# Feed-forward stages of a two-block transformer kernel: gate and up products with the weights stationary

## The reference, cut to what matters

```python
h = rms_norm(x, norm2_g[l])                      # x * rsqrt(mean(x^2) + eps) * g
x = x + (jax.nn.silu(h @ w_gate[l]) * (h @ w_up[l])) @ w_down[l]     # D_FF = 2816
```

## Time and profile before

| | us |
|---|---|
| three runs | 1618.80, 1624.56, 1621.87 |
| median | 1621.87 |
| the profiled execution, its own time | 1621.89 |
| its span, first to last instruction | 1620.1 |
| mean granted TensorE clock | 0.994 of full |

### The profile page before, as it was taken

One profiled execution on the slowest core, in us unless ns is written; L12 is line 12 of the kernel. 1 busy time (PEld: TensorE's weight loads), 2 busy tenths in 40 slices (PEclk: granted clock), 3 DMA queues, 4 the chain that ended last, 5 costly groups with the idle time before them and its releaser, 6 DMA issues.

```text
span 1620.1 us, 18657 instructions
## 1 busy us (share of the span) xinstructions
PE 1581.8 (98%) x7684; PEld 1312.0 (81%) x7684; DVE 1059.0 (65%) x1321; ACT 773.4 (48%) x887; POOL 29.1 (2%) x24
## 2 busy tenths in 40 slices
PE   8999999999999999899998999999999998999997
PEld 6888888888888888788886888888888886788886
DVE  5778565666875657955556876567955556875655
ACT  5645444456554445654344354445554444354443
POOL 0100000001000000000100000000000010000000
PEclk9999999999999999999999999999999999999999
DMA  8535555454355554444633454554543633365551
GB/s 306 180 107 198 189 197 186 156 192 146 132 206 184 195 189 161 180 156 133 167 130 113 168 188 182 185 195 166 204 150 134 149 130 130 132 219 182 184 195 63
DMA packets 54243, 273.78 MB, mean 169 GB/s; under 512 B 18704, under 2 KB 19344, under 8 KB 22160
## 3 DMA queue, kind: packets, MB, share of 16 engines
q1 hardware_dynamic: 40496, 268.05, 46.3%
q10 hardware_dynamic: 13664, 4.55, 2.0%
HBM read 271.53 MB, written 1.05 MB: 168 GB/s over the span
## 4 chain that ended last, share of the span: by engine, by line
PE 81%; DVE 11%; ACT 5%; issue 2%; DMA 0%; ACTq 0%; DVEq 0%; PEldq 0%
PE psum L391 24%; PE psum L393 24%; PE psum L392 24%; DVE wl L1211 5%; PE psum L431 3%; ACT wh L863 3%; PE psum L764 1%; PE psum L485 1%; DVE arena L1335 1%; PE psum L738 1%; ACT arena L1112 1%; PE psum L770 1%; DVE work L1300 1%; DVE arena L1293 1%; DVE work L1671 1%
## 5 line engine op out<-in xcount | busy, mean ns | idle before, releaser
L1211 DVE TENSOR_TENSOR wl<-raw,wh 128x2048 fp32r<-128x2048 f32 x250 | 573.6, 2298 | 424.8 <-ACT wh L863 421.6
L391 PE MATMUL psum<-wh,xh 128*128 128x512 f32 (+1 forms) x1632 | 648.4, 397 | 4.9 <-DVE work L1671 1.8
L393 PE MATMUL psum<-wh,xl 128*128 128x512 f32 (+1 forms) x1632 | 634.3, 389 | 0.0
L392 PE MATMUL psum<-wl,xh 128*128 128x512 f32 (+1 forms) x1632 | 633.3, 388 | 0.0
L863 ACT ACTIVATE wh<-raw 128x2048 fp32r<-128x2048 f32 x250 | 476.1, 1910 | 321.7 <-PE psum L393 315.2
L391 PEld LDWEIGHTS psum<-wh,xh 128*128 128x128 f32 x1632 | 308.0, 189 | 77.2 <-issue 19.3
L393 PEld LDWEIGHTS psum<-wh,xl 128*128 128x128 f32 x1632 | 307.6, 189 | 63.4
L392 PEld LDWEIGHTS psum<-wl,xh 128*128 128x128 f32 x1632 | 308.2, 189 | 58.0
L391 PE MATMUL psum<-wh,ah 128*128 128x512 f32 (+1 forms) x360 | 141.7, 394 | 6.4 <-DVE work L1671 6.4
L393 PE MATMUL psum<-wh,al 128*128 128x512 f32 (+1 forms) x360 | 140.9, 391 | 0.0
L392 PE MATMUL psum<-wl,ah 128*128 128x512 f32 (+1 forms) x360 | 140.8, 391 | 0.0
(11 more groups left out here) (156 smaller groups left out, 1075.2 us busy)
## 6 DMA issues: line engine op xcount, KB each, us to landing
raw<-in_weights SPq DMA_DIRECT2D x250, 1024.0 KB, 4.8
arena<-in_rpb ACTq DMA_DIRECT2D x32, 96.0 KB, 6.6
raw<-in_weights SPq DMA_DIRECT2D x8, 256.0 KB, 7.5
out<-arena SPq DMA_DIRECT2D x3, 256.0 KB, 3.0
x<-in_x SPq DMA_DIRECT2D x2, 256.0 KB, 3.5
x<-in_x ACTq DMA_DIRECT2D x2, 256.0 KB, 7.0
arena<-in_table_decay SPq DMA_DIRECT2D x1, 512.0 KB, 5.1
work<-in_masks SPq DMA_DIRECT2D x1, 512.0 KB, 5.2
```

The source lines that it names most:

```text
L391: nc.tensor.matmul(dst, lh, right(wh, slot), start=start, stop=False)
L392: nc.tensor.matmul(dst, lh, right(wl, slot), start=False, stop=False)
L393: return nc.tensor.matmul(dst, ll, right(wh, slot), start=False, stop=stop)
L1211: nc.vector.tensor_tensor(wl[:, slot, :], raw[:, slot, :], wh[:, slot, :].bitcast(F32), ALU.subtract).then_inc(split_ready.sem, 1)
```

## The change

- Gate and up are transposed. A 128 x 128 block of the weights is stationary and the tokens stream past: `wh` against `xh` and `xl` side by side (512 columns, two strips of 256 from the joint tile `xhl`, into the left and the right half of a bank), then `wl` against `xh` (256 columns, into the left half). The result is left plus right half, with hidden features on the partitions, in four chunks c: gate in the two PROJ banks, up in the two TR banks (for slice 0 in ACC+2 and ACC+3). The transposes and their bank are gone.
- The activation changes with it. ScalarE copies the gate's right halves, VectorE adds the left halves (which frees PROJ), multiplies by the norm's factor, ScalarE takes tanh, VectorE makes `(tanh + 1) * gate`; ScalarE copies the up halves, VectorE adds and multiplies. `ah` and `al` are made from the result in SBUF.
- The factor now varies along a row. VectorE builds diagonals from it, TensorE multiplies a matrix of ones by them (`rms_rows`, one f32 matmul of 256 columns inside `gate_up` of slice 0), and VectorE copies the row tile `rms_row`. The factor of the up product, with the 0.5, is applied after down, in `add_to_x` (`scaled=True`).
- Orders: VectorE does `split_low(F+3)` before `activate(0)`, ScalarE loads the tanh table with a one-element activation and does `split_high(F+3)` before the slice's copies; in each turn `act_high` and `act_low` come before the split of piece q+3.

The signal counts, the memset of `ones` and the changed calls are left out of this diff:

```diff
-xh = sb("xh", [P, KT, SEQ], F32R)
-xl = sb("xl", [P, KT, SEQ], F32R)
+xhl = sb("xhl", [P, 2, KT, SEQ], F32R)
+xh, xl = xhl[:, 0, :, :], xhl[:, 1, :, :]
...
-mlp_gate = part(work, 0, NT, 256)
-mlp_tanh = part(work, 1024, NT, 256)
-mlp_act = part(work, 1536, NT, 256)
+mlp_gate = part(work, 0, 2, SEQ)
+rms_row, rms_diag = part(work, 512, SEQ), part(work, 768, SEQ)
+mlp_tanh = part(work, 1024, 2, SEQ)
+mlp_act = part(work, 1536, 2, SEQ)
+mlp_up = part(work, 4096, 2, SEQ)
...
+def up_banks(i):
+    return TR if i else ACC + 2
+def halves(first):
+    return psum[:, first:first + 2, 0:SEQ], psum[:, first:first + 2, SEQ:2 * SEQ]
...
     def ffn(L, F, U, xl_groups, norm_n, after):
-        def gate_up(i, q, slot, groups=(None, None), between=None):
-            project(L, q, U + i, 0, last=False, slot=slot, left_ready=groups[0], between=between)
-            yield
-            project(L, q + 1, U + i, 4, first=False, slot=(slot + 1) % RING,
-                    left_ready=groups[1])
-        def act_t(i):
-            pe.wait_ge(*a_ready.by(L, i + 1))
-            for kk in range(2):
-                for t in range(NT):
-                    mm = nc.tensor.transpose(bank(TR)[:, kk * SEQ + t * P:kk * SEQ + (t + 1) * P],
-                                             mlp_act[:, t, kk * P:(kk + 1) * P], ident[:, :])
-            mm.then_inc(at_full.sem, 1)
+        def gate_up_half(i, q, k0, slot, groups=None, between=None):
+            pe.wait_ge(*split_ready.by(L, q + 1))
+            for c in range(4):
+                if k0 == 0 and c % 2 == 0:
+                    pe.wait_ge(*proj_free[c // 2].by(L, U + i))
+                if (i, k0, c) == (1, 0, 2):
+                    pe.wait_ge(*tr_free.by(L, norm_n + 4))
+                dst = bank((up_banks(i) if c >= 2 else PROJ) + c % 2)
+                for kk in range(4):
+                    if groups is not None and c == 0 and kk % 2 == 0:
+                        pe.wait_ge(*xl_ready.by(L, groups + kk // 2 + 1))
+                    cols = slice(kk * 512 + c * P, kk * 512 + (c + 1) * P)
+                    nc.tensor.matmul(dst, wh[:, slot, cols], xhl[:, :, k0 + kk, :],
+                                     start=(k0, kk) == (0, 0), stop=False, skip_group_check=True)
+                    mm = nc.tensor.matmul(dst[:, 0:SEQ], wl[:, slot, cols], xh[:, k0 + kk, :],
+                                          start=False, stop=(k0, kk) == (4, 3), skip_group_check=True)
+                if c == 1:
+                    if k0 == 4:
+                        mm.then_inc(proj_full[0].sem, 1)
+                    if between:
+                        between()
+            mm.then_inc(piece_used.sem, 1)
+        def gate_up(i, q, slot):
+            gate_up_half(i, q, 0, slot)
+            gate_up_half(i, q + 1, 4, (slot + 1) % RING)
+        def rms_rows():
+            pe.wait_ge(*diag_ready.by(L, 1))
+            nc.tensor.matmul(bank(ACC)[:, 0:SEQ], ones[:, :], rms_diag, start=True, stop=True)\
+                .then_inc(row_full.sem, 1)
...
-            act_t(i)
...
+                pe.wait_ge(*proj_free[1].by(L, U + FFI))
...
         def turn(i, q, start):
-            g = gate_up(i, q, (F + 2) % RING)
-            next(g)
-            act_t(i - 1)
-            for _ in g:
-                pass
+            gate_up(i, q, (F + 2) % RING)
             down(i - 1, q + 2, (F + 4) % RING, start)
-        for _ in gate_up(0, F, F % RING, (xl_groups - 4, xl_groups - 2),
-                         lambda: norm_operand(L, norm_n, 4, (2, 3))):
-            pass
+        gate_up_half(0, F, 0, F % RING, xl_groups - 4, lambda: norm_operand(L, norm_n, 4, (2, 3)))
+        gate_up_half(0, F + 1, 4, (F + 1) % RING, xl_groups - 2, rms_rows)
         turn(1, F + 2, True)
         for i in range(2, FFI - 1):
             turn(i, i * 3 + (F - 1), False)
         last = FFI - 1
-        g = gate_up(last, F + 29, (F + 29) % RING)
-        next(g)
-        act_t(last - 1)
-        for _ in g:
-            pass
+        gate_up(last, F + 29, (F + 29) % RING)
         last_downs(last, F + 31)
...
-    def ffn(L, F, U, rms_n, after):
-        def gate_tanh(i, full1):
-            for t in range(NT):
-                act.wait_ge(*(full1 if t else proj_full[0].by(L, U + i + 1)))
-                nc.scalar.activation(mlp_tanh[:, t, :], bank(PROJ + t)[:, 0:256], ACT.Tanh,
-                                     scale=rms[:, 6 + t:7 + t]).then_inc(tanh_ready.sem, 1)
+    def ffn(L, F, U, after):
+        def gate_half(i):
+            act.wait_ge(*proj_full[0].by(L, U + i + 1))
+            nc.scalar.activation(mlp_gate, halves(PROJ)[1], ACT.Copy).then_inc(gate_low.sem, 1)
+        def gate_tanh(i):
+            act.wait_ge(*gate_ready.by(L, i + 1))
+            nc.scalar.activation(mlp_tanh, mlp_gate, ACT.Tanh, scale=0.5).then_inc(tanh_ready.sem, 1)
+        def up_half(i, q):
+            act.wait_ge(*used(L, q + 1))
+            nc.scalar.activation(mlp_up, halves(up_banks(i))[1], ACT.Copy).then_inc(up_low.sem, 1)
+        def gate_up(i, q):
+            gate_half(i)
+            gate_tanh(i)
+            up_half(i, q)
         def act_high(i, high=ah, k0=0):
-            act.wait_ge(*at_full.by(L, i + 1))
-            nc.scalar.activation(high[:, k0:k0 + 2, :], part(bank(TR), 0, 2, SEQ), ACT.Copy)\
-                .then_inc(ah_ready.sem, 1)
+            act.wait_ge(*a_ready.by(L, i + 1))
+            nc.scalar.activation(high[:, k0:k0 + 2, :], mlp_act, ACT.Copy).then_inc(ah_ready.sem, 1)
         def turn(i, q, turns):
             s = (F + 2) % RING
+            act.wait_ge(*used(L, q - 1))
+            act_high(i - 1)
             split_high_at(L, q + 3, s, turns + (F + 5) // RING)
-            act_high(i - 1)
-            gate_tanh(i, used(L, q + 1))
+            gate_up(i, q)
             split_high_at(L, q + 4, (s + 1) % RING, turns + (F + 6) // RING)
             split_high_at(L, q + 5, (s + 2) % RING, turns + (F + 7) // RING)
-        act.wait_ge(*rms_ready.by(L, rms_n))
-        gate_tanh(0, used(L, F + 1))
+        nc.scalar.activation(one_tanh[:, :], one_root[:, :], ACT.Tanh)
         split_high(L, F + 3)
+        gate_up(0, F)
         split_high(L, F + 4)
         turn(1, F + 2, 0)
         for i in range(2, FFI - 1):
             turn(i, i * 3 + (F - 1), i - 1)
+        act.wait_ge(*used(L, F + 28))
+        act_high(FFI - 2)
         split_high(L, F + 32)
-        act_high(FFI - 2)
-        gate_tanh(FFI - 1, used(L, F + 30))
+        gate_up(FFI - 1, F + 29)
         if after is None:
...
-    def add_to_x(L, waits, first=0):
+    def add_to_x(L, waits, first=0, scaled=False):
         for j in range(first, first + len(waits)):
             n, t = j // 2, j % 2
             v.wait_ge(*waits[j - first])
             xs = x[:, t, n * 512:(n + 1) * 512]
-            nc.vector.tensor_tensor(xs, bank(ACC + j), xs, ALU.add).then_inc(x_ready.sem, 1)
+            if scaled:
+                ins = nc.vector.scalar_tensor_tensor(xs, bank(ACC + j), rms[:, 6 + t:7 + t], xs,
+                                                     ALU.mult, ALU.add)
+            else:
+                ins = nc.vector.tensor_tensor(xs, bank(ACC + j), xs, ALU.add)
+            ins.then_inc(x_ready.sem, 1)
     def ffn(L, F, U, after):
         def activate(i):
-            for t in range(NT):
-                v.wait_ge(*tanh_ready.by(L, i * NT + t + 1))
-                step.wait(L, nc.vector.tensor_scalar(mlp_gate[:, t, :], bank(PROJ + t)[:, 0:256],
-                                                     rms[:, t:t + 1], None, ALU.mult))
-                nc.vector.scalar_tensor_tensor(
-                    mlp_act[:, t, :], bank(PROJ + t)[:, 256:512], rms[:, 6 + t:7 + t],
-                    mlp_gate[:, t, :], ALU.mult, ALU.mult).then_inc(proj_free[t].sem, 1)
+            v.wait_ge(*gate_low.by(L, i + 1))
+            nc.vector.tensor_tensor(mlp_gate, halves(PROJ)[0], mlp_gate, ALU.add)\
+                .then_inc(proj_free[0].sem, 1)
+            v.wait_ge(*proj_free[0].by(L, U + i + 1))
+            nc.vector.tensor_tensor(mlp_gate, mlp_gate, rms_row.unsqueeze(1).to_broadcast([P, 2, SEQ]),
+                                    ALU.mult).then_inc(gate_ready.sem, 1)
+            v.wait_ge(*tanh_ready.by(L, i + 1))
+            nc.vector.scalar_tensor_tensor(mlp_act, mlp_tanh, 1.0, mlp_gate, ALU.add, ALU.mult)
+            v.wait_ge(*up_low.by(L, i + 1))
+            nc.vector.tensor_tensor(mlp_up, halves(up_banks(i))[0], mlp_up, ALU.add)\
+                .then_inc(proj_free[1].sem, 1)
             v.wait_ge(*proj_free[1].by(L, U + i + 1))
-            nc.vector.scalar_tensor_tensor(mlp_act, mlp_tanh, 1.0, mlp_act, ALU.add, ALU.mult)\
-                .then_inc(a_ready.sem, 1)
+            nc.vector.tensor_tensor(mlp_act, mlp_act, mlp_up, ALU.mult).then_inc(a_ready.sem, 1)
         def act_low(i, high=ah, low=al, k0=0):
             v.wait_ge(*ah_ready.by(L, i + 1))
```

(47 more changed lines are left out.)

## The result

The changed kernel takes 1632.19 us (median of 5 runs, 1628.99 to 1634.78), before 1622.86 (median of 5). The ratio is 1.005, 95% interval 1.0036 to 1.0065: slower by 0.5%, where I had forecast 1619.5 with a range to 1628.0. The profiled execution has a span of 1630.4 us against 1620.1.

What follows compares the result with a forecast made beforehand. TensorE's own stream was taken to bound the kernel. Against the profiled 1621.89 us, -21.2 (transposes) + 8.5 (more matmuls) + 9.2 (stage starts) + 1.1 (stage ends) = -2.4 gave 1619.5 us; range 1610.5 to 1628.

Steps and rivals of the forecast that it cites:

- What bounds the kernel: Whole kernel: TensorE is busy 98% of the span, and its own stream sets the time within a feed-forward stage.
- Term 1: Each turn: four transposes vanish, 0.48 us for each of 44 sets, 21.2 us gained.
- Term 2: Gate and up: 16 more, shorter matmuls a slice at 13.3 ns each, 8.5 us lost; bounds 0 and 8.5.
- rival A: Gate and up: narrow matmuls cost their columns alone, the 8.5 us loss goes, 1611.0 us; chance 12%.
- The strips: Wide matmuls in gate and up: reading the moving operand from two strips costs 0; upper bound 13.3 ns each.
- Rival C: Gate and up: two strips make each of 1280 wide matmuls 13.3 ns slower, 17.0 us, 1636.5 us; chance 10%.
- Term 3: Start of each stage: turn 1 waits for slice 0's gate sum, starts 2.3 us later; 9.2 us lost in all.
- Term 4: End of each stage: 4.6 us against 4.83, with 0.48 already booked as gain; 1.1 us lost in all.
- B: Start of each stage: the wait is absent or much smaller (0.4 us), 1611.9 us; chance 7%.
- D: Start of each stage: ScalarE pauses 1.28 us after the table load, delaying the start, 1624.6 us; chance 3%.
- E: Inside turns: VectorE delivers `wl` or `al` late, a turn stays at 16.80 us, 1632.2 us in all; chance 4%.

Runs made afterwards that it cites:

- the layout side by side: Changed kernel with the joint tile laid out so the high and low parts of each block of x are contiguous: 1632.04 us, ratio 1.005 to before.
- the last experiment: Changed kernel with slice 0's activation ahead of the split of piece F+3, and matmuls ordered for few width changes: 1612.73 us, ratio 0.9945 to before.
- groups of four: Changed kernel with four wide matmuls, then four narrow ones in a chunk, instead of wide and narrow in turn: 1625.96 us (one run).
- all wide: Changed kernel with the low weights also streamed against both parts of x, so no narrow matmul is left: 1755.75 us (one run).
- halves: Kernel before, old orientation, with the middle matmul of each gate and up product cut into two of 256 columns: 1629.24 us (one run).
- no transposes: Kernel before with the four transposes of each slice left out: 1599.62 us (one run), beside 1620.02 for before.
- slice 0 first: Changed kernel with slice 0's activation ahead of the split of piece F+3 on ScalarE and VectorE: 1619.24 us, ratio 0.9981 to before.

## Why the prediction was wrong, point by point

**What bounds the kernel**: right. TensorE's stream sets the time within the stages, and the changes of its steps and waits came through to the end.

**Term 1, the transposes**: right, 21.2 us forecast, 20.4 (by the traces 22.4) by leaving them out.

**Term 2, more and shorter matmuls**: this is the step that failed, by its size. "One line fits all three: 0.4168 ns a column and 13.3 ns a matmul", and with it 0.213 us a slice and 8.5 us in all. The line was made from runs of equal width. Between widths it does not hold: behind a run of narrow matmuls the first five wide ones are slower by 1 to 9 ns, and with the two in turn every wide one is, by 6 to 14 ns, and the first ten of the down behind them nearly all. The turn grew by 16.79 - 16.32 = 0.47 us in place of 0.21, so by the turns the term is 40 x 0.47 = 18.8 us, and it eats the gain of term 1. My rows even had the effect: I put "the slower matmuls behind them" into the transposes' price and did not ask whether another short matmul would do the same. I had taken the upper bound of the rows for the worst case, and it was not one. I said of rival A that no narrow matmul stands between wide ones in the trace; the same gap had to open the range on the other side.

**The strips**: 0, as taken. Rival C has the sign and, net, half of the size (slow wide matmuls), but its cause is wrong, as the layout side by side shows. Its condition, over 5.6 ns a wide matmul, came true at 6.1 ns a pair.

**Term 3, the start**: right to a tenth (2.39 against 2.3), with the chain as forecast. What the forecast lacked is a term for what came with it: as the wait ended the clock fell in 2 of 4 starts, 1.5 to 1.7 us each. In the trace of before TensorE stands idle for 0.32 us at most in a stage, and I did not ask what a wait of 2 us does to the clock.

**Term 4, the end**: right (4.52 against 4.6).

**Sum**: per stage the forecast had 2.3 - 2.67 - 0.2 = -0.6, measured is +1.7. Of that difference, 2.27 a stage or 9 us in all is term 2 (stage 1, from turn 1 to the last gate/up: -0.40 where -2.67 was forecast), and 3.2 us in all is the clock: 1619.5 + 9 + 3.2 = 1631.7, measured 1632.2. By the turns alone term 2 is off by 18.8 - 8.5 = 10.3 us; what makes up the 1.2 us between this and the 9 stays open.

**The rivals**: A is out: a narrow matmul takes 0.120 us among its like in the last experiment and 0.117 on average in the pairs, never the 0.107 of its columns alone, and the wide ones beside it got slower. With A goes the constant of the Trainium skill (TensorE: Matmul & The Clock Gate, "Back-to-back issue gap"), which the page gives for the isolated gap: the trace disagrees with its 2.5 ns after the change as before. B is out, the wait is there. D is out: the activation starts 0.02 us behind the table load. The drain that the Trainium skill adds (ScalarE: Activation LUTs, "What ACT_TABLE_LOAD costs") is in no trace here. E has the number (turn 16.80, 1632.2) with the wrong engine: VectorE is never late inside a turn, TensorE itself is slower. That the whole time agrees too is luck, since E has nothing for the 3.2 us of the clock. A price in the right place with a wrong cause would have led to a wrong mend; the order of the matmuls is the right one.

## What to carry to other kernels

When matmuls change width, take the step from rows where the two widths stand side by side, and where there are none, keep the range open on the costly side. Order the matmuls so that equal widths stand together as long as the banks allow. When the work that frees a bank is moved behind a weight split on another engine, count the whole chain to the matmul that needs it: here a swap of two lines on each of two engines was worth 13 us.

## What the runs showed of the hardware that I had not expected

- A 512-column fp32r matmul takes 0.2267 us behind its like, but 233, 236, 228, 233 and 231 ns as the first to the fifth behind a run of 256-column ones (medians over the last experiment's trace); the first narrow one behind a run of wide ones takes 113 ns where 120 is normal. Behind wide and narrow in turn the effect lasts longer: the first ten of the down take 241, 237, 233, 236, 224, 231, 236, 228, 232 and 231 ns (the changed kernel). A return to wide costs 20 ns net if five or more wide ones follow, 6 ns if only one does. What in TensorE makes it is open: no run told a cause in the weight loads from one in the matmuls themselves.
- The clock: in the three traces with the wait of over 2 us at each start (the changed kernel, side by side, groups of four) it fell to 1.2 GHz at or within 2 us of the wait's end in 4 of 12 starts. In the six traces without that wait (before, all wide, halves, no transposes, slice 0 first, few changes) it fell at none of 24 starts. Why one such wait brings it down and the next doesn't is open. The same traces have a longer wait to compare: twice in each, in the attention stages of the second kind of layer, TensorE stands idle for 3.2 us, and in all 18 cases the clock fell within 1.3 us of that wait's end. The work around those waits is another, so the length of the wait isn't shown to be the cause.
- The one-element activation right behind a table load starts 0.01 us after the load ends (11 to 12 ns, 0.02 us in the rounded rows above, at all 24 starts of a stage in the changed kernel and the five variants of it).
